# One seven-product stage for both output products, with the final norm's rows staged in DRAM

## Chip, cores and metric

One core of a Trainium2 chip runs the whole program. The metric is device microseconds of one execution; lower is better. All matrices are float32; a factor of a product is split into a high part (rounded to float32r) and a low part, and a product is the sum of high x high, high x low and low x high.

## The reference, cut to what matters

For 1024 prompt tokens and 32 sample tokens (T = 1056 columns; D_MODEL = 2048), the last steps of the layer and of the trunk are

```python
mixed = jnp.concatenate([att * jax.nn.silu(ga), ssm * jax.nn.silu(gs)], axis=-1)
h = h + mixed @ w_out                        # 2048 x 2048
e = _rmsnorm(pe @ w_pe, g_pe)                # made earlier, unscaled, kept as eT in DRAM
h = h + e * jax.nn.sigmoid(h @ w_pg)         # 2048 x 2048
y = _rmsnorm(h, g_final)                     # over the 2048 features of each token
```

Earlier stages (input projection, attention, state space, the embedding's product and the GLU) are not changed.

## The kernel before

Activations lie feature-major: a panel is 128 features by 1056 tokens. Engines run their own instruction lists and wait for each other's semaphores; each list is in the written order, DMA queues included.

**stage_mix** (line 2578) makes h = x + mixed @ w_out. The 2048 input features are halved in two groups of eight *passes* (`NPM` = 8), each group using one half, and each pass makes one pair of 128-row blocks of h (256 output features, `mix_pair`). Inside a pass the 2 x 2 block product (features in two quarters of 512, tokens in two halves of 528) is made as seven block products in place of eight, with sums of weight blocks (`sums`) and of activation blocks. One block product (`product`, line 2751) is 4 x 3 x 2 = 24 matmuls of 264 columns, into the PSUM regions X, B and Y. The seven *sides* (activation factors, 128 x 2112 each) lie split in `m_t_act`; the seven weight factors of a pass are made on the fly in a ring of four. In the loops over `p` (pass) and `j` (slot, 0 to 6) ScalarE casts factor n + 3 (`high`), VectorE makes its sum n + 4 and its low part n + 3 (`sums`, `low`), and both empty PSUM regions (`seed_*`, `keep_*`, `drain_*`, `u2`, `c11`, `c22`, `c12`).

Passes 0 to 7 are opening: they leave partial blocks in `m_zb`, SP stores six of the eight pairs to `cT`. Passes 8 to 15 are closing: they take the partial blocks up again (POOL's `load_part`, line 2722), `residual` adds x from `m_x_res` in four steps, and POOL's `store_h` writes h to `hT`. POOL also moves the *rides*: for the second half of the features, rows of mixT come to `m_ride`, VectorE subtracts (`subtract_rides`), and the differences are stored to `tS`. At the change from pass 7 to 8 POOL reloads each side as soon as its last product is over (`reload_side`), ScalarE casts it (`high_side`, slot n + 3) and VectorE makes its low part (`low_side`, slot n + 4).

**stage_output** (line 3048) has the tokens in two parts, 0 to 511 and 512 to 1055. All 16 panels of h of a part are kept split (`h_hi`, `h_lo`). For each of 16 output tiles of w_pg TensorE runs 16 x 3 matmuls per chunk (`tile`, line 3182; one chunk of 512 columns in part 0, two of 272 in part 1). ScalarE takes the sigmoid, VectorE `gate` scales e by g_pe and e_rstd, multiplies and adds h (rejoined by POOL from the two parts), TensorE transposes the tile (`turn`), ScalarE sums squares (`squares`), VectorE writes it with g_final to token rows (`fill`). When a part is through, `tail` makes rstd, scales the rows and they are stored: part 0's while part 1 computes, part 1's at the very end.

Of the kernel before, what the change touches and what calls it, by code (L numbers as in the profile page):

```python
# [61 lines left out]
RING_H, EARLY_H = 6, 6  # L62
# [50 lines left out]
class Weights:  # L113


    def __init__(self, sb, sem, name, kt, shared=None, before=0):


        self.kt, self.kh, self.before = kt, kt // 2, before
        self.raw, loaded = shared or ([sb(f"{name}_raw{h}", [P, self.kh, P]) for h in range(2)], None)  # L120
        self.hi = [sb(f"{name}_hi{b}", [P, kt, P], F32R) for b in range(2)]
        self.lo = [sb(f"{name}_lo{b}", [P, kt, P], F32R) for b in range(2)]
        self.loaded = loaded or [sem(f"{name}_loaded{h}") for h in range(2)]
# [11 lines left out]
    def split_tile(self, dve, nc, n, b, in_use):  # L135
# [3 lines left out]
        for h in range(2):  # L139
            dve.wait_ge(self.loaded[h], (n + (self.before + 1)) * 16)  # L140
            nc.vector.tensor_copy(self.hi[b][:, h * self.kh:(h + 1) * self.kh], self.raw[h][:]) \
              .then_inc(self.hi_done, 1)
# [5 lines left out]


def prefetch(sp, shared, w, col):  # L150

    raw, loaded = shared
    kh = KD // 2
    for h in range(2):
        sp.dma_start(raw[h][:], w[0].rearrange("(k p) n -> p k n", p=P)[:, h * kh:(h + 1) * kh, col:col + P]) \
          .then_inc(loaded[h], 16)
# [2412 lines left out]

def mix_count(p):  # L2570
    return 16 * (p - NPM + 1)


def mix_pair(p):
    return (p + KEPT) % NPM if p < NPM else p - NPM


def stage_mix(nc, d, G):


    with ExitStack() as ctx:  # L2581
        sb, ps, sem = allocators(nc, ctx)
        pad = sb("m_pad", [P, P // 2])
        t_act, w_raw = sb("m_t_act", [P, 7, 2, KQ, HN], F32R), G["m_raw"]
        W, out = G["W"], G["out"]
        s3 = sb("m_s3", [P, KQ, P])
        w_hi = [sb(f"m_hi{s}", [P, KQ, P], F32R) for s in range(RING_W)]
        w_lo = [sb(f"m_lo{s}", [P, KQ, P], F32R) for s in range(RING_W)]
        zb = [sb(f"m_zb{b}", [P, 4, HN]) for b in range(2)]
        x_res, ride = sb("m_x_res", [P, 4, HN]), sb("m_ride", [P, 4, HN])  # L2590
        acc = ps("m_acc", [P, 6, 512])
# [3 lines left out]
        raw_loaded = {**G["m_blocks"], **{n: sem(f"m_{n}_loaded") for n in ("b12_again", "b22", "b21")}}  # L2595
# [7 lines left out]
            sem(f"m_{n}") for n in ("added", "ridden", "x_loaded", "h_added", "order"))  # L2603
        z_stored = [sem(f"m_z_stored{b}") for b in range(2)]
# [3 lines left out]
        RELOADED = [MOVED + 16 * (1 + n) for n in (2 * NRIDE, NRIDE, NRIDE, 0, NRIDE, 0, NRIDE)]  # L2608
        block = ctx.enter_context(nc.Block(no_gpsimd_drain=True))

        w_out = d["w_out"][0].rearrange("(k p) n -> p k n", p=P)
        mixT = d["mixT"].rearrange("(k p) t -> p k t", p=P)
        hT = d["hT"].rearrange("(k p) t -> p k t", p=P)
        last = 2 * NPM - 1
        DONE = ((0, c11_done), (3, c22_done), (1, c12_done), (2, c21_done))

        def block_of(panel, kh, th):
# [873 lines left out]
```

## Time and profile before

| | us |
|---|---|
| median of 3 runs (2363.88 to 2371.13) | 2366.49 |
| the profiled execution | 2364.5 |
| its span | 2362.5 |
| stage_mix, first to last product | 1583.2 to 1932.9 |
| stage_output, first matmul to last product's end | 1935.8 to 2334.4 |
| after it, to the end of the span | 28.1 |
| TensorE busy, of the span | 93% |
| VectorE, ScalarE, GpSimd busy | 68%, 38%, 13% |

Times inside the profile are counted from the start of the span. The profiled execution's own time is 2.0 us more than its span. TensorE's granted clock has two levels, 2.4 GHz (1.00 in the rows) and 1.2 GHz (0.50), and a stretch shows their mean. Busy time of matmuls overlaps, since they are pipelined: the distance between starts is what one costs.

### The profile page before, as it was taken

What the parts mean: (1) busy time and instruction counts of PE and PEld (TensorE: products, weight loads), DVE (VectorE), ACT (ScalarE), POOL (GpSimd) and SP (SyncE); (2) the same over time, 40 slices, a digit from 0 to 9 for tenths busy, and PEclk for the clock granted to TensorE, in tenths of its full rate; (3) what the DMA queues carried; (4) which work ended last, traced back from release to release, by engine and by line L of the source; (5) the groups of instructions that cost most, each with busy time, mean ns of one, the idle gap of its engine ahead of it and who ended that gap; (6) DMA issues with size and microseconds to landing.
All of it is one profiled execution on the core that took longest, in us unless ns stands there. A gap on an engine that the chain in (4) does not pass through costs nothing. (4 is left out here: it accounts for less than half of the span.)

```text
span 2362.5 us, 44125 instructions
## 1 busy us (share of the span) xinstructions
PE 2202.1 (93%) x16355; PEld 2110.7 (89%) x16355; DVE 1615.5 (68%) x2941; ACT 904.8 (38%) x1843; POOL 315.2 (13%) x412
## 2 busy tenths in 40 slices
PE   3999999999999999999789978978999999999995
PEld 3899999999999999999778868978999988889995
DVE  6779766767787887886456646667566566666663
ACT  6442333333533333334366736234353331123112
POOL 0011000000011212111153410001101211111110
PEclk7999999999999999999989989989999999999998
DMA  8484444444657878786377655464554675445332
GB/s 247 139 269 113 145 139 124 151 124 142 217 182 207 233 215 238 209 242 166 113 245 222 205 181 182 129 207 150 205 195 162 219 246 164 116 118 185 105 97 98
DMA packets 360527, 416.14 MB, mean 176 GB/s; under 512 B 75744, under 2 KB 294472, under 8 KB 352992
## 3 DMA queue, kind: packets, MB, share of 16 engines
q1 hardware_dynamic: 306096, 263.34, 37.9%
q0 software_dynamic: 28224, 106.10, 13.1%
q10 hardware_dynamic: 26032, 44.35, 5.7%
q8 instruction: 112, 1.84, 0.3%
q14 instruction: 63, 0.52, 0.1%
HBM read 265.68 MB, written 139.35 MB: 171 GB/s over the span
## 5 line engine op out<-in xcount | busy, mean ns | idle before, releaser
L767 PE MATMUL acc<-t_act,w_hi 128*128 128x264 f32 x5376 | 886.6, 287 | 9.1 <-DVE zb L1329 5.8
L767 PEld LDWEIGHTS acc<-t_act,w_hi 128*128 128x128 f32 x5376 | 747.4, 189 | 15.5 <-issue 14.1
L767 PE MATMUL acc<-t_act,w_lo 128*128 128x264 f32 x2688 | 547.8, 285 | 0.0
L767 PEld LDWEIGHTS acc<-t_act,w_lo 128*128 128x128 f32 x2688 | 417.0, 189 | 0.0
L2777 PE MATMUL m_acc<-m_t_act,m_hi 128*128 128x264 f32 x1792 | 296.4, 288 | 14.2 <-ACT m_acc L2820 9.8
L1322 DVE TENSOR_TENSOR w_lo<-w_raw_f,w_hi 128x512 fp32r<-128x512 f32 x288 | 197.9, 687 | 133.9 <-ACT w_hi L977 133.5
L977 ACT CAST w_hi<-w_raw_f 128x512 fp32r<-128x512 f32 x288 | 177.9, 618 | 267.7 <-PE acc L767 239.2
L2777 PEld LDWEIGHTS m_acc<-m_t_act,m_hi 128*128 128x128 f32 x1792 | 253.0, 191 | 15.1 <-issue 14.9
L3191 PE MATMUL post_acc<-h_hi,w_post_hi 128*128 128x272 f32 (+1 forms) x768 | 211.2, 329 | 5.7 <-PEq L2581 2.8
L3191 PE MATMUL post_acc<-h_hi,w_post_lo 128*128 128x272 f32 (+1 forms) x768 | 209.0, 327 | 0.0
L3191 PE MATMUL post_acc<-h_lo,w_post_hi 128*128 128x272 f32 (+1 forms) x768 | 208.4, 326 | 0.0
L2777 PE MATMUL m_acc<-m_t_act,m_lo 128*128 128x264 f32 x896 | 184.4, 287 | 0.0
L3191 PEld LDWEIGHTS post_acc<-h_hi,w_post_hi 128*128 128x128 f32 x768 | 130.3, 191 | 17.7 <-DVE h_lo L3292 3.2
L2777 PEld LDWEIGHTS m_acc<-m_t_act,m_lo 128*128 128x128 f32 x896 | 140.7, 191 | 0.0
L3191 PEld LDWEIGHTS post_acc<-h_lo,w_post_hi 128*128 128x128 f32 x768 | 130.1, 191 | 11.0
L3191 PEld LDWEIGHTS post_acc<-h_hi,w_post_lo 128*128 128x128 f32 x768 | 129.3, 190 | 11.3
L2951 DVE TENSOR_TENSOR m_lo<-m_raw,m_hi 128x512 fp32r<-128x512 f32 x96 | 66.0, 688 | 56.3 <-ACT m_hi L2804 56.3
L3245 ACT ACTIVATE junk<-y_ps 128x128 f32<-128x128 f32 (+1 forms) x144 | 37.0, 274 | 172.7 <-PE y_ps L3179 172.7
L3306 DVE TENSOR_TENSOR h<-h,gate_sig 128x512 f32<-128x512 f32 (+1 forms) x32 | 22.7, 709 | 108.5 <-ACT gate_sig L3238 108.5
L661 POOL DMA_DIRECT2D zT<-zb x80 | 43.3, 542 | 342.2 <-DVE zb L1338 145.5
L3141 POOL TENSOR_TENSOR total<-h_hi,h_lo 128x512 f32 (+3 forms) x32 | 50.0, 1565 | 287.3 <-DVE h L3309 277.0
L2804 ACT CAST m_hi<-m_raw 128x512 fp32r<-128x512 f32 x96 | 59.2, 620 | 64.4 <-PE m_acc L2777 61.2
(435 smaller groups left out, 3620.0 us busy)
## 6 DMA issues: line engine op xcount, KB each, us to landing
w_raw_f<-in_w_in_dram SPq DMA_DIRECT2D x96, 512.0 KB, 4.0
w_raw<-in_w_pg_dram SPq DMA_DIRECT2D x64, 512.0 KB, 4.7
cT<-zb SPq DMA_DIRECT2D x22, 1056.0 KB, 4.3
zb<-cT POOLq DMA_DIRECT2D x88, 264.0 KB, 6.2
zT<-zb POOLq DMA_DIRECT2D x80, 264.0 KB, 3.6
m_raw<-in_w_out_dram SPq DMA_DIRECT2D x32, 512.0 KB, 5.6
eT<-e_out ACTq DMA_DIRECT2D x16, 528.0 KB, 3.1
m_x_res<-xT SPq DMA_DIRECT2D x8, 1056.0 KB, 6.2
```

The costliest lines, as they stand in the source:

```text
L661: pool.dma_start(d["zT"][row:row + P, tok:tok + HN], zb[b][:, i]).then_inc(z_put[i], 16)
L767: mm = pe.matmul(out[:, c, 0:QN], w[:, k, :], t_act[:, SIDE[r], x, k, c * QN:(c + 1) * QN], start=(opens and k == 0 and m == 0), stop=(k = ...
L977: nc.scalar.copy(w_hi[n % RING_W][:], factor(p, r)).then_inc(hi_done, 1)
L1322: TT_(w_lo[n % RING_W][:], factor(n // 7, n % 7), w_hi[n % RING_W][:].bitcast(F32), ALU.subtract) \
L2777: mm = pe.matmul(out[:, c, 0:QN], w[:, k, :], t_act[:, MSIDE[r], x, k, c * QN:(c + 1) * QN], start=(opens and k == 0 and m == 0), stop=(k ...
L2804: nc.scalar.copy(w_hi[n % RING_W][:], factor(p, r)).then_inc(hi_done, 1)
L2951: TT_(w_lo[n % RING_W][:], factor(n // 7, n % 7), w_hi[n % RING_W][:].bitcast(F32), ALU.subtract) \
L3141: nc.gpsimd.tensor_tensor(total[b][:, 0:WIDTH[part]], row(hi, part, m).bitcast(F32), row(lo, part, m).bitcast(F32), ALU.add).then_inc(tota ...
L3191: mm = pe.matmul(acc[b][:, c, 0:width], w[:, k, :], a[:, k, start:start + width], start=(k == 0 and n == 0), stop=(k == KD - 1 and n == 2))
L3245: s = nc.scalar.activation(junk[0:rows, t], tr_ps[b][0:rows, t * P:(t + 1) * P], ACT.Square, accum_out=ssq[0:rows, t, bass.ds(m, 1)])
L3306: nc.vector.tensor_tensor(h2[b][:, 0:w], h2[b][:, 0:w], sig[b][:, 0:w], ALU.mult).then_inc(e_gated, 1)
```

## The change

`stage_output` is gone. `stage_mix` runs 32 passes: 0 to 15 as before with w_out, 16 to 23 opening and 24 to 31 closing with w_pg and sides made of h (`block_of`: mixT for c < 2, hT above). The opening and closing roles follow `mix_opens(p)`.

- The sides change three times (before passes 8, 16 and 24). For the latter two `high_side` stands in slot n + 4 and `low_side` in n + 5. Rides happen in passes 1 to 4, 11 to 14 and 17 to 20, and are loaded and stored by SP instead of POOL; `subtract_rides` stands in slot 6.
- h sums go to `x_res`, which is doubled, and hT is stored from there, not from `zb`. The block X of a closing pass comes to its own buffer `x_part`. `load_part` and `store_h` go block by block, in turn.
- In passes 16 to 23 e is loaded, scaled by g_pe and e_rstd (`scale_e`) and stored back to eT; in passes 24 to 31 it is loaded again with h as residual.
- In passes 24 to 31 the four blocks get a sigmoid, a multiply and an add (`gate`); nine token tiles of 256 features are turned in five steps, three to six slots later (`turn`, `squares`, `fill`). The rows of the first six pairs go to `yS` in DRAM (`store_tiles`, ScalarE's queue) and come back in two DMAs in the last pass; those of the last two stay in SBUF.
- All nine token tiles are scaled and stored at the end, five by VectorE and SP, four by ScalarE.
- At the start of the stage `seed_y(0)` stands before the last three sides; the difference for side 6 is made in slot 1 from a second copy of the block, and sides 4, 5, 6 are split in slots 0, 1, 3. The first w_pg tile is no longer loaded ahead into a shared buffer.

```diff
-                    if p == 0 and j < 3:
-                        low_side(4 + j, 4 + j)
+                    if p == 0 and j == 0:
+                        low_side(4, 4)
+                    if p == 0 and j == 1:
+                        dve.wait_ge(raw_loaded["b21_again"], 16)
+                        TT_(first_side[6], ride[:], first_side[2], ALU.subtract).then_inc(t_sub, 1)
+                        low_side(5, 5)
+                    if p == 0 and j == 3:
+                        low_side(6, 6)
...
-                    for s in range(7):
-                        if 7 * p + j == 7 * (NPM - 1) + s + 4:
-                            low_side(7 + s, s)
+                    for c in range(1, 4):
+                        for s in range(7):
+                            if 7 * p + j == 7 * (c * NPM - 1) + s + (4 if c == 1 else 5):
+                                low_side(7 * c + s, s)
...
+                    if 2 * NPM <= p < GATE and j == 5:
+                        scale_e(p)
+                    if p > GATE and j < 2:
+                        gate(p - 1, j + 1)
+                    if p > GATE and j == 1:
+                        gate(p - 1, 3)
+                    if p > GATE + 1 and j < 2:
+                        fill(p - 2, j + 3)
+                    if p > GATE and j >= 4:
+                        fill(p - 1, j - 4)
+                    if p >= GATE and j == 6:
+                        gate(p, 0)
...
+            def turn(p, f):
+                at = fill_at(p, f)
+                pe.wait_ge(h_added, done_count(p, 2 if f < 2 else 3))
+                if at >= 2:
+                    pe.wait_ge(y_filled, at - 1)
+                    pe.wait_ge(squared, at - 1)
+                x = x_res[p % 2].rearrange("p (m h) t -> p m (h t)", m=2)
+                for a, t in enumerate(FILLS[f]):
+                    rows = tile_rows(t)
+                    for m in range(2):
+                        tr = pe.transpose(oth[0:rows, at % 2, (2 * a + m) * P:(2 * a + m + 1) * P],
+                                          x[:, m, t * P:t * P + rows], ident[:])
+                tr.then_inc(turned, 1)
+
+            for p in range(4 * NPM):
                 for r in range(7):
+                    if p > GATE and r >= 3:
+                        turn(p - 1, r - 3)
+                    if p > GATE + 1 and r == 0:
+                        turn(p - 2, 4)
                     product(p, r)
...
+            for s in range(7):
+                reload_side(1, s)
             for p in range(NPM, 2 * NPM):
+                if p == 2 * NPM - 1:
+                    reload_side(2, 0)
+                    reload_side(2, 1)
+                if NPM + KEPT <= p + 1 < 2 * NPM:
+                    load_part(p + 1, 3)
+                for n in range(4):
+                    if NPM + KEPT <= p + 1 < 2 * NPM and n < 3:
+                        load_part(p + 1, n)
+                    if p > NPM:
+                        store_h(p - 1, n)
+            for s in range(2, 7):
+                reload_side(2, s)
...
+            for g in range(3):
+                sp.wait_ge(tiles_put[g], 16 * (NPM - 2))
+            for k, r in ((0, 1), (3, 4)):
+                sp.wait_ge(prod_done, 7 * last + r + 1)
+                sp.dma_start(y_all[:, k:k + 3].rearrange("p k t c -> p k (t c)"),
+                             d["yS"][k:k + 3].rearrange("k p x -> p k x")).then_inc(y_back, 16)
```

## Rows read from the trace of the kernel before

**Rows 1.** The page's busy times, share of the span, instructions: TensorE and VectorE.
```profile
PE 2202.1 (93%) x16355; PEld 2110.7 (89%) x16355; DVE 1615.5 (68%) x2941; ACT 904.8 (38%) x1843; POOL 315.2 (13%) x412
```
**Rows 2.** The page's chain that ended last, shares of the span by line.
```profile
PE post_acc L3191 16%; PE m_acc L2777 12%; PE y_ps L3179 1%; DVE m_t_act L2905 0%; DMA m_t_act<-mixT 0%; ACT m_t_act L2791 0%; DVE m_lo L2951 0%; DMA hT<-m_zb 0%; DVE h_lo L2991 0%; DVE m_zb L3008 0%; DVE w_post_lo L146 0%; DVE m_ride L3004 0%; POOL out_dram L3108 0%; DVE h_lo L3292 0%; ACT junk L3245 0%
```
**Rows 3.** Windows: both stages, the side change, a closing pass, the last stores.
```profile
core 0: us, PE busy (x) PEld busy (x) DVE busy (x) ACT busy (x) POOL busy (x), PEclk, DMA share, GB/s
1583.20:1932.90 349.70, 335.53 (x2690) 334.45 (x2689) 231.42 (x311) 133.87 (x208) 45.84 (x84) 0.97 0.56 193
1935.80:2334.40 398.60, 392.31 (x2443) 355.52 (x2443) 248.39 (x296) 78.74 (x340) 53.27 (x36) 0.98 0.43 130
1748.00:1770.00 22.00, 21.52 (x175) 21.16 (x174) 16.63 (x17) 17.35 (x19) 3.52 (x6) 1.00 0.95 362
...
1824.00:1846.00 22.00, 22.00 (x182) 22.00 (x181) 13.29 (x21) 6.82 (x12) 4.30 (x8) 1.00 0.60 207
2343.30:2355.00 11.70, 0.00 (x0) 0.00 (x0) 1.01 (x1) 1.77 (x1) 1.03 (x2) 0.50 0.98 378
```
**Rows 4.** Waits from 1583 to 1936 us: who for whom, total, times, longest.
```profile
ACT m_acc L2809 <- DMA m_zb<-cT: 25.3, 6, 5.2
...
PE m_acc L2777 <- ACT m_acc L2820: 9.8, 1, 9.8
...
PE m_acc L2777 <- DVE m_zb L2958: 3.9, 1, 3.9
...
PE post_acc L3191 <- PEq L2581: 2.8, 1, 2.8
```
**Rows 5.** Groups by form, 1933 to 2362.5 us: busy, mean ns, idle before.
```profile
L3321 DVE TENSOR_TENSOR y_tok<-y_ps,g_bc 128x512 f32 x24 | 16.6, 692 | 24.6 <-ACT junk L3245 24.6
```
**Rows 6.** Groups by form, 1758 to 1933 us: the sides and the casts.
```profile
L2804 ACT CAST m_hi<-m_raw 128x512 fp32r<-128x512 f32 x47 | 28.9, 620 | 32.3 <-PE m_acc L2777 32.3
...
L2905 DVE TENSOR_TENSOR m_t_act<-m_t_act 128x2112 fp32r<-128x2112 f32 x7 | 16.5, 2350 | 0.0
...
L2791 ACT CAST m_t_act<-m_t_act 128x2112 fp32r<-128x2112 f32 x5 | 9.8, 1970 | 1.7 <-DMA m_t_act<-mixT 1.7
```
**Rows 7.** Timelines at the side change: TensorE, then VectorE (start, duration, what).
```profile
1778.55 0.72 PE L2777 MATMUL m_acc<-m_t_act,m_hi 128*128 128x264 f32 x4 [3.88 <-DVE m_zb L2958]
...
1780.75 1.08 PE L2777 MATMUL m_acc<-m_t_act,m_hi 128*128 128x264 f32 x4
...
1783.78 0.65 PE L2777 MATMUL m_acc<-m_t_act,m_hi 128*128 128x264 f32 x4
...
1775.43 2.35 DVE L2905 TENSOR_TENSOR m_t_act<-m_t_act 128x2112 fp32r<-128x2112 f32 x1
1777.70 0.70 DVE L2958 TENSOR_TENSOR m_zb<-m_acc,m_zb 128x528 f32<-128x528 f32 x1
1778.32 0.68 DVE L2951 TENSOR_TENSOR m_lo<-m_raw,m_hi 128x512 fp32r<-128x512 f32 x1
```
**Rows 8.** Timeline of TensorE where part 0 ends and part 1 begins.
```profile
2126.12 0.39 PE L3191 MATMUL post_acc<-h_hi,w_post_hi 128*128 128x512 f32 x1
2126.35 0.39 PE L3191 MATMUL post_acc<-h_lo,w_post_hi 128*128 128x512 f32 x1
...
2128.56 0.41 PE L3191 MATMUL post_acc<-h_lo,w_post_hi 128*128 128x272 f32 x2
2128.81 0.41 PE L3191 MATMUL post_acc<-h_hi,w_post_lo 128*128 128x272 f32 x2
```
**Rows 9.** Timeline of the tail: rstd, and VectorE's three scaled tiles.
```profile
2340.42 0.19 DVE L3339 RECIPROCAL rstd_y<-std_y 128x5 f32<-128x5 f32 x1 [0.29 <-ACT std_y L3251]
...
2340.65 3.67 DVE L3343 TENSOR_SCALAR y_tok<-y_tok,rstd_y 128x2048 f32<-128x2048 f32 x3
```
**Rows 10.** DMA issues from 1748 to 1802 us: size, median us to landing.
```profile
m_t_act<-tS POOLq DMA_DIRECT2D x4, 1056.0 KB, 7.4
```

More of the change, by code:

```diff
@@ L2660, in load_w, with put_landed @@
                     sp.wait_ge(s_done, 4 * p)
[L2661 to L2662 removed]
+                s, k, col = raw_slot(p, h), p // NPM % 2 * 2 * KQ + h * KQ, mix_pair(p) * 2 * P
+                w = w_out if p < 2 * NPM else w_pg
+                sp.dma_start(w_raw[s][:], w[:, k:k + KQ, col:col + 2 * P]).then_inc(w_loaded[s], 16)
+            def put_landed(p):
+                for i in range(4):
+                    sp.wait_ge(z_put[i], PUT + mix_count(p))
@@ L2688, in _ @@
-            for b in range(2):
-                sp.wait_ge(z_stored[b], 16 * (NPM - KEPT) // 2)
+                    load_residual(NPM)
+                    load_residual(NPM + 1)
+                    with nc.allow_non_contiguous_dma("per-feature columns of the gain"):
+                        sp.dma_start(g_pe[:], d["g_pe"][0].rearrange("(k p) -> p k", p=P)).then_inc(gains_loaded, 16)
+                if ride_of(p - 1):
+                    store_ride(*ride_of(p - 1))
+                if NPM + 2 <= p < 2 * NPM:
+                    put_landed(p - 2)
+                    load_residual(p)
@@ new lines, in _ @@
+                    if p > GATE and j == 0:
+                        sigmoid(p - 1, 2)
+                    if p > GATE + 1 and j == 0:
+                        squares(p - 2, 4)
+                    if p > GATE and j >= 3:
+                        squares(p - 1, j - 3)
+                    for g, (q, slot) in enumerate(((1, 6), (2, 1), (2, 2))):
+                        if GATE <= p - q < last - 1 and j == slot:
+                            store_tiles(p - q, g)
+                    for c in range(1, 4):
+                        for s in range(7):
+                            if 7 * p + j == 7 * (c * NPM - 1) + s + (3 if c == 1 else 4):
+                                act.wait_ge(sides_moved[s], reloaded(c))
+                                high_side(7 * c + s, s)
@@ L3022, in _ @@
                         c22(p)
-                    if p == last and j == 6:
-                        for k in range(EARLY_H):
-                            low_h(k)
                     if j == 6:
@@ new lines, in _ @@
+            fill(last - 1, 3)
+            gate(last, 1)
+            gate(last, 2)
+            fill(last - 1, 4)
+            gate(last, 3)
+            for f in range(5):
+                fill(last, f)
+            nc.vector.reduce_sum(var[:], ssq[:], axis=AX_X).then_inc(var_summed, 1)
+            dve.wait_ge(var_summed, 1)
+            nc.vector.tensor_scalar(var[:], var[:], 1.0 / D_MODEL, EPS, ALU.mult, ALU.add).then_inc(var_done, 1)
+            dve.wait_ge(std_done, 1)
+            nc.vector.reciprocal(rstd[:], std[:]).then_inc(rstd_done, 1)
```

764 lines of the change are left out of this document (313 added, 451 removed).

## The prediction

> **What bounds the kernel now.** I read first the page's busy times, then its chain of waits: TensorE is busy 93% of the span, and the chain that ended last is mostly TensorE, 16% of the span on line 3191 (the product with w_pg) and 12% on line 2777 (the product with w_out) [rows 1, 2]. Then the stages [rows 3]. The seven-product stage runs from 1583.2 to 1932.9 us, the w_pg stage from 1935.8 to 2334.4, and after it 28.1 us of tail hold almost no TensorE work. In both stages TensorE is busy 96 to 98% of the time at a granted clock of 0.97 to 0.98 (2.4 GHz most of the time), so fewer matmul columns mean less time until something else is late. The waits [rows 4] and the two timelines [rows 7, 9] give what that costs where it already happens.
>
> **The product itself.** Before: part 0 is 16 tiles x 48 matmuls of 512 columns, 768, which start 0.231 us apart (0.23 and 0.23 between the rows); part 1 is 16 x 96 = 1536 of 272 columns, two in 0.25 us, 0.1255 each [rows 8]. That is 177.4 + 192.8 = 370.2 us. 144 transposes at about 0.12 us (five start within 0.6, an estimate from a 128-wide matmul's share of the 272-wide one's 0.1255) are 17, and the remaining 11 of the stage's 398.6 are its start at the low clock and waits for h_lo.
> After: 16 passes of 7 products of 24 matmuls of 264 columns. In a pass of the stage before, 182 matmuls start in 22 us [rows 3] (the row 1824 to 1846), one per 0.121 to 0.122. A pass is 168 x 0.1222 = 20.5 us, a product ("slot" below) 2.93, sixteen passes 328.5. The same 144 transposes are there, but 126 fall between products (18 a pass in the last seven), and the last 20 in the tail: 14 us. Together 342.5. The idle 2.8 us between the blocks goes as well [rows 4]. So TensorE's part falls by 398.6 + 2.8 - 342.5 = 58.9 us. Everything below takes back from this.
>
> **Two more changes of the side operands.** Each new group of eight passes reloads seven sides of 1056 KB; each costs ScalarE 1.97 us and VectorE 2.35 [rows 6]. The trace has one such change, at pass 8: the seven VectorE pieces, 16.5 us, put it behind, and TensorE stood 3.9 us until u2 was done [rows 4, 7]; then groups of four matmuls took 1.08 us in place of 0.65 for about 4 us [rows 7], about 2 us more. So one change costs 6 to 6.5 us today, and the kernel keeps that one. At the two new ones low_side stands a slot later (n + 5, before n + 4), so a side is finished two slots before its product and not three. Counting VectorE by starts (0.60 to 0.62 us from one 512 or 528 wide operation to the next, 2.27 after a side, where the durations are 0.68, 0.70 and 2.35 [rows 7]):
> At pass 16 the slots from (15,5) to the c22 of (16,5) hold seven sides 15.9, seven lows 4.3, four sums 2.4, two evacuations 1.4, four residuals 2.5 and that c22 0.7, 27.2 us, against eight slots, 23.4 us. Product 6 is 3.8 us late, with the clock about 6. Four POOL stores of h now stand between the side loads, which also wait for the last ride store, and ride, x, h and side bytes together are about 11.9 MB in a pass of 20.5 us, while the one change seen ran at 0.95 DMA share and 362 GB/s [rows 3]. I take 8, bounds 4 (the late products hidden as partly as at pass 8) and 15 (the loads late by three slots).
> At pass 24 there are also scale_e (two 1056-wide operations, 2.6 in all, an estimate from the 0.70 of a 528-wide one [rows 7]), add_parts 1.9, u2 and c11 1.4, and no residual: 30.7 us for the same eight slots, 7.2 late. The gaps come in several pieces, each with a stretch at the low clock: I take 11, bounds 6 and 22 (twice what I count, if ScalarE, which waits in order for a side's landing of 7.4 us [rows 10], holds back its casts and so VectorE).
> Of TensorE's clock the Trainium skill says the same in "TensorE: Matmul & The Clock Gate" ("HAM oscillation"): each return to work after an idle stretch is paid at the lower clock. Our rows agree (3.9 us idle, then about 4 us of 1.08 us groups); by that rule many pauses of a few us would be dearer than one of their sum, and it is the reason for the upper bound.
>
> **The eight passes with the gate.** Per pass VectorE gets: seven lows 4.3, four sums 2.4, four evacuations 2.5, four gates of two operations 5.2, and fills of nine row tiles 2.9 (512-wide 0.69 [rows 5], the 256-wide ones about 0.4). 17.3 us of a pass of 20.5 + 2.0. ScalarE: seven casts 4.3 (0.62 each [rows 6]), evacuations and seeds 3.0, three sigmoids 1.8, squares about 3.5, 12.6 in all. Neither is full. Slot by slot: slots 0 and 1 carry two and four gate halves more than they have room for (about 2.6 us behind at the end of slot 1), slot 2 has one operation, and u2 of slot 3 is in time. Transposes f + 2 wait for fill f, which ends 2.6 to 2.8 us into a slot of 2.93 + 0.5. So nearly no stall, but it's tight: I take 2 us, bounds 0 and 20 (0.6 us at each of 35 turns).
> DMA of a gate pass: w 1.05, h 1.08, e 1.08, cT 1.08 and staged rows 1.18 MB, 5.5 MB in 22.5 us, 243 GB/s; a pass now runs at 207 with a share of 0.60 [rows 3], so 0.7. Nothing there. Passes 17 to 20 (w, cT, e in and out, rides in and out) need 6.4 MB, 312 GB/s, share 0.9. scale_e may wait there a few us; it is last in its slot, low is three slots ahead, so nothing for TensorE.
> The split of residual and hT stores (x_res doubled, x_part) removes a wait of ScalarE for cT, 25.3 us over six [rows 4]. In the steady passes TensorE was full already [rows 3]: nothing gained. The rides move from POOL to SP: SP waits there for things that are done by slot 4, its weight loads have seven slots; nothing.
>
> **The start.** TensorE waits 9.8 us for seed_y of pass 0, queued behind a high_side that waits for the third difference [rows 4]. Now seed_y is ahead, and two of the 2112-wide VectorE operations come behind products 3 and 4. Laid out by VectorE durations, product 6 of pass 0 ends 3.8 us earlier, but the one gap becomes four of 0.5 to 2.4, some at the low clock. I take -2, bounds -5 and +3.
>
> **The tail.** Today 6.0 us from the last matmul to rstd, then scaling, and the data flow from 2343.3 to 2355.0 at 378 GB/s: 4.46 MB, rows 512 to 1055 [rows 3, 9]; the others were stored at half time under matmuls. Then 7.5 us to the end. Afterwards all 8.65 MB go out at the end: 4.19 MB more at 378 is 11.1 us. rstd comes later by about 3.3: the last gate half, then five chained turn, squares and fill steps in two banks in place of one. The scaling isn't the bound: VectorE makes a tile in 1.22 us [rows 9]. The reload of six passes' rows, 7.1 MB, begins when product 1 of the last pass is over and ends about when rstd does. The new block ends without the GpSimd drain, -2. Sum +12, bounds +6 (the 7.5 us mostly go) and +20 (reload late by 6, 300 GB/s).
> The Trainium skill, "DMA: Bandwidth & Descriptors" ("Where 436 GB/s comes from"), lets about 358 GB/s of HBM traffic bind. The row has 378; by the page the extra bytes would take 11.7 us, 0.6 more.
>
> **Sum.** -58.9 + 8 + 11 + 2 - 2 + 12 = -27.9 us. The profiled execution took 2364.5 us (span 2362.5), so 2336.6; it lies 2.0 below the median of 2366.49, so I give 2338.
>
> **The rivals.**
> A. Everything at its lower bound: the changes hide as the one at pass 8 does, and the end overhead goes. -58.9 + 4 + 6 + 0 - 5 + 6 = -48, 2318. For it: nothing else than TensorE is above 68% busy. Against: VectorE is over its slots by count at both changes.
> B. DMA holds the changes and the tail: both upper bounds, 15 + 22, and 20 for the tail: -58.9 + 37 + 2 - 2 + 20 = -2, 2364, no change; half of that, 2352. For it: 0.95 share at the change seen. Against: that change cost only 3.9 us though the queues were full.
> C. Slower: the order between TensorE and VectorE in the gate passes. Product r stands behind turn f, turn behind fill f - 2, fill behind a low that waits for ScalarE's cast, which stands behind squares and sigmoids. If one such round trip misses its slot, all do: TensorE then waits in each of 35 turns, and falls to 1.2 GHz for stretches. At 0.8 us a turn it costs 28 us and the gain is gone; at 1.2 us, 42, 2378. For it: 2.8 of 3.4 us used by my count. Against: slots 2 and 3 leave VectorE about 2 us of room each pass.
> D. The change doesn't do what it says, sixteen passes but with products held at 1.2 GHz or passes far over 22.5 us for another reason: no row speaks for it; part of C.
>
> **How the numbers follow.** My forecast, 2328 to 2348: 0.48. A, below 2328: 0.15. B, 2348 to 2359: 0.18 faster, 0.06 no change. C: 0.13, of which 0.12 slower and 0.01 no change. Within 0.3% is 2359.4 to 2373.6, about what a measurement of this kernel can tell from none. Faster 0.81, same 0.07, slower 0.12. The range 2316 to 2364 leaves out a part of A and nearly all of C.
>
> **What would show it.** TensorE's passes 16 to 31 at 20.5 us, and 22.5 with turns; idle of 3 to 8 us once near the start of each of passes 16 and 24, ahead of r = 4 to 6, released by VectorE; the first wait of 9.8 us replaced by three short ones; from the last product to the first store 11 to 13 us and then some 23 us of full DMA. Wrong would be: waits of transposes on the gate or fill in every pass, idle at the changes released by DMA, or TensorE time per pass above 23.

## The result and the profile after

The changed kernel takes 2376.26 us (median of 4 runs, 2374.82 to 2378.66), the kernel before 2365.18 beside it (4 runs, 2363.42 to 2371.13): ratio 1.0044, 95% interval 1.0027 to 1.0062. It is slower, by 11 us; the forecast was 2338 and the range ended at 2364. The profiled execution took 2374.8 us, its span is 2373.1.

The page of the kernel after, busy times and the chain that ended last; they answer to [rows 1, 2]:
```profile
PE 2172.8 (92%) x16739; PEld 2110.0 (89%) x16739; DVE 1652.8 (70%) x3049; ACT 1001.8 (42%) x1862; POOL 269.0 (11%) x387
...
PE 14%; DMA 7%; DVE 7%; issue 2%; SPq 2%; ACT 1%; POOL 0%; ACTq 0%; DVEq 0%; POOLq 0%
PE m_acc L2930 13%; DMA tS<-m_ride 3%; DMA m_ride<-hT 2%; SPq L2761 2%; DVE m_t_act L3135 2%; DVE m_lo L3181 1%; DMA m_ride<-mixT 1%; PE m_oth L2945 1%; DMA m_t_act<-tS 1%; DVE m_zb L3151 1%; DVE m_s L3172 0%; DMA m_e_res<-eT 0%; ACT m_y_out L3121 0%; DVE m_ride L3141 0%; DVE m_ride L3142 0%
```
TensorE is still busy 92% of the span. But in the chain its share fell, and right behind its own line stand the two ways of a ride, `tS<-m_ride` and `m_ride<-hT`, and SP's issue of the ride's stores (SPq L2761). None of these three stands among the lines that the chain of before shows, and the forecast had given them nothing.

The windows of the kernel after, for [rows 3]: passes 0 to 15, passes 16 to 31, then passes 3 to 5, 14 and 15, 16, 19 to 22, 24, the gate pass 26, and the last stores (most windows lie up to 2 us behind the first product of their pass; after the times: busy us of each engine, TensorE's granted clock, DMA share, GB/s):
```profile
core 0: us, PE busy (x) PEld busy (x) DVE busy (x) ACT busy (x) POOL busy (x), PEclk, DMA share, GB/s
1585.00:1952.80 367.80, 342.85 (x2702) 339.01 (x2702) 237.39 (x321) 134.73 (x205) 36.03 (x65) 0.97 0.59 203
1952.80:2336.84 384.04, 350.33 (x2801) 346.85 (x2800) 273.77 (x384) 168.78 (x351) 20.19 (x37) 0.98 0.70 256
...
1656.90:1733.10 76.20, 67.33 (x510) 66.36 (x509) 38.83 (x58) 20.81 (x37) 0.00 (x0) 0.93 0.56 190
1905.40:1952.80 47.40, 42.86 (x340) 41.53 (x339) 32.83 (x49) 14.01 (x22) 9.57 (x17) 1.00 0.76 262
1952.80:1987.50 34.70, 23.31 (x171) 22.41 (x170) 26.28 (x25) 19.34 (x21) 2.90 (x6) 0.90 0.76 294
2029.00:2133.80 104.80, 88.31 (x676) 86.81 (x675) 62.22 (x85) 27.54 (x48) 0.00 (x0) 0.95 0.68 245
2154.30:2181.80 27.50, 21.67 (x170) 20.76 (x169) 26.79 (x28) 16.64 (x21) 0.43 (x1) 1.00 0.66 245
2204.30:2227.00 22.70, 22.70 (x190) 22.68 (x189) 17.79 (x30) 12.01 (x35) 2.14 (x4) 1.00 0.69 250
2350.00:2366.00 16.00, 0.00 (x0) 0.00 (x0) 4.06 (x4) 6.14 (x4) 0.00 (x0) 0.50 1.01 417
```
What the reader is to see: passes 3 to 5 moved only 190 GB/s at a DMA share of 0.56, and still took some 76 us where three plain passes take 61.7. A closing pass of the kernel before moved 207 GB/s without a loss [rows 3], so the bytes alone don't explain it; run 3 tries order against bytes. The gate pass has no idle TensorE at all.

Each pass by the starts of its products. A plain pass took 20.55 us, a gate pass 22.47; all 5376 product matmuls are in the trace, so a pass is known to 0.1. The account in spans, after less before, beside the terms of the forecast:

| term | forecast | measured |
|---|---|---|
| the product, worked out again from nine passes of 20.55 and seven of 22.47 | -58.9 | -59.2 |
| start (pass 0) | -2 | -3.8 |
| passes 3 to 5 (28.4, 26.1, 21.4), rides of change 1 | 0 | +14.2 |
| passes 14 and 15 (24.1, 23.1) | 0 | +6.2 |
| pass 16 (34.7), second change of sides | +8 | +14.2 |
| passes 19 to 22 (30.0, 26.0, 25.5, 23.1), rides of change 3 | 0 | +22.5 |
| pass 24 (27.5), third change of sides | +11 | +7.0 |
| turns and gates | +2 | 0 |
| tail, from the last product's end | +12 | +8.0 |
| passes 7 and 8, and a later start of the stage | 0 | +1.8 |
| sum | -27.9 | +10.9 (spans: +10.6) |

How a ride makes a pass long. VectorE's and SP's waits in passes 1 to 5 of the kernel after:
```profile
DVE m_raw L3163 <- DMA m_raw<-in_w_out_dram: 23.0, 5, 5.6
DVE m_ride L3140 <- DMA m_ride<-mixT: 21.3, 3, 10.7
...
SPq L2785 <- DVE m_zb L3152: 79.0, 6, 15.2
SPq L2752 <- DMA tS<-m_ride: 9.4, 3, 4.4
```
And SP's and VectorE's timelines (start, duration, what, idle before):
```profile
1673.58 0.33 SPq L2785 DMA_DIRECT2D cT<-m_zb  x1
1674.00 0.38 SPq L2740 DMA_DIRECT2D m_raw<-in_w_out_dram  x1
1674.43 4.55 SPq L2761 DMA_DIRECT2D tS<-m_ride  x4
1679.02 1.02 SPq L2740 DMA_DIRECT2D m_raw<-in_w_out_dram  x1
1683.04 0.81 SPq L2752 DMA_DIRECT2D m_ride<-mixT  x2
...
1666.16 0.71 DVE L3140 TENSOR_TENSOR m_ride<-m_ride 128x528 f32<-128x528 f32 x1 [10.68 <-DMA m_ride<-mixT]
1690.52 0.71 DVE L3140 TENSOR_TENSOR m_ride<-m_ride 128x528 f32<-128x528 f32 x1 [6.02 <-DMA m_ride<-mixT]
1713.64 0.71 DVE L3140 TENSOR_TENSOR m_ride<-m_ride 128x528 f32<-128x528 f32 x1 [4.59 <-DMA m_ride<-mixT]
```
A ride is a closed ring through one buffer. From one difference to the next: 2.9 us of differences, 4.5 until SP may issue the cT store, which waits for add_parts of the next pass (line 3152), 0.9 for cT and a weight load, 4.6 for the issue of the four stores, 4.1 with the next weight load until they have landed, 0.8 for two loads, and 6.7 until VectorE goes on: 24.4 us between 1666.16 and 1690.52, against a plain pass of 20.55. From the first difference of one ride to that of the next the trace has 31.3, 24.4 and 23.1 us in change 1, 24.3, 24.0 and 24.1 in change 2, and 31.0, 25.8 and 25.7 in change 3. VectorE stands in slot 6 for what is missing; behind it in its order are `sums` and `low` of the coming products, so TensorE stands too, and part of the 23.0 us for the weights is the same stall, since their loads are issued behind those stores.

### The profile page after: what moved, and what is told of

The parts are those of the page before. It is cut to its first block and busy times, and to the rows that moved or that the text cites. A ratio compares the mean times of both kernels' runs of the same rounds, so it can differ in the third digit from the quotient of the medians.

```text
span 2373.1 us, 44712 instructions
## 1 busy us (share of the span) xinstructions
PE 2172.8 (92%) x16739; PEld 2110.0 (89%) x16739; DVE 1652.8 (70%) x3049; ACT 1001.8 (42%) x1862; POOL 269.0 (11%) x387
## 2 busy tenths in 40 slices
DMA packets 331078, 477.63 MB, mean 201 GB/s; under 512 B 78912, under 2 KB 250280, under 8 KB 321088
## 5 line engine op out<-in xcount | busy, mean ns | idle before, releaser
L757 PEld LDWEIGHTS acc<-t_act,w_hi 128*128 128x128 f32 x5376 | 749.1, 189 | 15.5 <-issue 14.2
L2930 PE MATMUL m_acc<-m_t_act,m_hi 128*128 128x264 f32 x3584 | 599.8, 290 | 58.7 <-DVE m_lo L3181 14.7
L2930 PEld LDWEIGHTS m_acc<-m_t_act,m_hi 128*128 128x128 f32 x3584 | 507.1, 192 | 65.9 <-issue 34.2
L2930 PE MATMUL m_acc<-m_t_act,m_lo 128*128 128x264 f32 x1792 | 369.7, 288 | 0.0
L2930 PEld LDWEIGHTS m_acc<-m_t_act,m_lo 128*128 128x128 f32 x1792 | 282.8, 192 | 0.0
L2978 ACT CAST m_hi<-m_raw 128x512 fp32r<-128x512 f32 x192 | 118.8, 620 | 174.8 <-PE m_acc L2930 101.8
L3181 DVE TENSOR_TENSOR m_lo<-m_raw,m_hi 128x512 fp32r<-128x512 f32 x192 | 131.4, 687 | 56.4 <-ACT m_hi L2978 56.3
L2244 DVE CUSTOM_DVE_ANT_0 prob<-score,negc_bc 128x128 f32<-128x128 f32 (+8 forms) x72 | 53.4, 750 | 30.8 <-PE score L2017 29.5
L2268 DVE TENSOR_TENSOR pt_lo<-turned,pt_hi 128x512 fp32r<-128x512 f32 (+2 forms) x112 | 52.8, 508 | 27.2 <-ACT pt_hi L2160 25.4
L2149 ACT ACTIVATE prob<-prob,stat 128x128 f32<-128x128 f32 (+8 forms) x72 | 56.1, 781 | 21.8 <-DVE stat L2244 14.9
L3135 DVE TENSOR_TENSOR m_t_act<-m_t_act 128x2112 fp32r<-128x2112 f32 x23 | 54.1, 2352 | 0.0
```

The costliest lines, as they stand in the source:

```text
L757: mm = pe.matmul(out[:, c, 0:QN], w[:, k, :], t_act[:, SIDE[r], x, k, c * QN:(c + 1) * QN], start=(opens and k == 0 and m == 0), stop=(k = ...
L2149: e = nc.scalar.activation(prob[s % 4][:, col:col + width], prob[s % 4][:, col:col + width], ACT.Exp, scale=-1.0, bias=stat[b][:, n, 0:1], ...
L2244: z = nc.vector.tensor_tensor_reduce(out=prob[s % 4][:, col:col + width], in0=score[b][:, col:col + width], in1=negc[hb][:, row:row + widt ...
L2268: c = nc.vector.tensor_tensor(out, src, hi.bitcast(F32), ALU.subtract)
L2930: mm = pe.matmul(out[:, c, 0:QN], w[:, k, :], t_act[:, MSIDE[r], x, k, c * QN:(c + 1) * QN], start=(opens and k == 0 and m == 0), stop=(k ...
L2978: nc.scalar.copy(w_hi[n % RING_W][:], factor(p, r)).then_inc(hi_done, 1)
```

## The experiments

Every ratio is against the kernel before in the same rounds. Where nothing else is said, a base is the changed kernel.

**1. no_rides.** Rides of changes 1 and 3 left out.
```diff
-        FIRST_RIDE = {1: 1, 2: NPM + 3, 3: 2 * NPM + 1}
+        FIRST_RIDE = {2: NPM + 3}
```


> Leaves out the rides of the first and third side change (no loads, no four differences, no stores to tS; sides 1, 2, 4, 6 of passes 8 to 15 and 24 to 31 are then not the right ones); those of the second stay. The changed kernel lost 14 us in passes 3 to 5 and 22 us in passes 19 to 22 against 20.55 us a pass. Theory 1 (the chain of one ride, subtract in slot 6, add_parts, cT store, weight load, four stores issued by SP, landing, two loads, landing, takes longer than a pass): both groups fall to 20.6 us a pass, -34 us, 2342. Theory 2 (too many bytes for the DMA queues): the same here, -34. Theory 3 (e's way out and back is what holds passes 19 to 22): only -14, 2362.


Measured: 2338.3 us, 0.9878 (0.9862 to 0.9895). Passes 3 to 5 and 19 to 22 are all at 20.55. The 36.7 us of the two groups are the rides.

**2. pool_rides.** Those rides through POOL, which loads, waits for the difference and stores; the differences stay in slot 6.
```diff
+            for r in range(NRIDE):
+                move_rides(1, r)
```


> The rides of the first and third change go through POOL's queue, as they did for the first change in the kernel before; the same bytes, and the differences stay in slot 6. Theory 1: a ride's chain loses the wait behind add_parts, the cT store and the weight load, and the 4.6 us that SP takes to issue four stores; it becomes 3 (differences) + 2.2 + 5 + 1.1 + 5 = 16 us, under a pass of 20.5: -25 to -34 us, 2342 to 2351. Theory 2 (bytes): nothing, 2376. Theory 3: -14.


Measured: 2353.4, 0.9942 (0.9925 to 0.9959). Off SP's queue, the rides cost 23 us less than in the changed kernel: pass 2 at 24.5, 3 at 21.3, 19 to 21 at 22.5, 23.5, 21.6. What is left is no longer a wait for a ride: before each first difference VectorE now stood 0.0 us. From 1638 to 1685 us it stood 12.5 us for two weight loads, 7.1 us for one of them; they landed 12.5 us (median) after their issue, beside the two residuals (13.4). So without SP's queue the ring no longer holds VectorE. The 11 us that these passes still lose look like transfers that crowd one another, a share of the bytes; that wasn't tried by itself.

**3. sp_shift.** The differences in slot 2 of the next pass, the stores behind the weight load that follows; still SP.
```diff
                 load_w(p + 2, 0)
+                if ride_of(p - 1) and ride_of(p - 1)[0] in (1, 3):
+                    store_ride(*ride_of(p - 1))
...
-                    if j == 6 and ride_of(p):
+                    if j == 6 and ride_of(p) and ride_of(p)[0] not in (1, 3):
                         subtract_rides(*ride_of(p))
+                    if j == 2 and ride_of(p - 1) and ride_of(p - 1)[0] in (1, 3):
+                        subtract_rides(*ride_of(p - 1))
```


> The rides of the first and third change stay in SP's queue, but the differences move from slot 6 of the pass to slot 2 of the next and the stores stand behind the next weight load instead of before x, e and that load. Same bytes, same queue. Theory 1: the chain is 3 + 4.6 + 4 + 0.8 + 6.5, 19 to 20 us, just under a pass, and a late ride meets a slot with room: -20 to -30 us, 2346 to 2356. Theory 2: nothing, 2376. Theory 3: -14.


Measured: 2349.4, 0.993 (0.9913 to 0.9946), 27 us less than the changed kernel with the same instructions and bytes. Passes 3 to 5 come to 20.6. Its VectorE timeline at the first difference of each ride has no more waits after the first:
```profile
1671.50 0.71 DVE L3142 TENSOR_TENSOR m_ride<-m_ride 128x528 f32<-128x528 f32 x1 [3.63 <-DMA m_ride<-mixT]
...
1688.40 0.70 DVE L3142 TENSOR_TENSOR m_ride<-m_ride 128x528 f32<-128x528 f32 x1
...
1708.96 0.70 DVE L3142 TENSOR_TENSOR m_ride<-m_ride 128x528 f32<-128x528 f32 x1
```
The bytes and the queue are the same, and the bytes theory had said 2376: it is refuted for these passes. Slot 2 of the next pass is also where the kernel before had its differences. The move of the differences and the move of the stores were not tried apart. One wait of 6 us was left, and pass 19 took 27.7.

**4. no_e.** scale_e and the way of e to eT and back left out in passes 16 to 23.
```diff
-                    if 2 * NPM <= p < GATE and j == 5:
-                        scale_e(p)
```


> Leaves out scale_e and e's load and store in passes 16 to 23 (e then goes unscaled into the gate); 2.16 MB and 2.5 us of VectorE less per pass. Theory 1: passes 19 to 22 keep most of their 22 us, since the ride chain is unchanged, and pass 24 gets 2 to 3 us shorter: -3 to -8 us, 2368 to 2373. Theory 2 (bytes): 6.4 MB a pass become 4.3, the 22 us go: -25, 2351. Theory 3: the same, -25; passes 3 to 5 are unchanged in every theory.


Measured: 2364.0, 0.9987 (0.9977 to 0.9998), 12 us less, between theory 1 (3 to 8) and the other two (25). Passes 20 to 23 fall to 20.5 to 21.0, pass 19 only from 30.0 to 28.9, passes 3 to 5 by 1.1 us in all, pass 24 from 27.5 to 25.1. So 13.6 of the 22.5 us in passes 19 to 22 appear only with e, more than theory 1 gave. The differences of change 3 still follow one another at 28.8, 23.1 and 21.6 us, where they had 31.0, 25.8 and 25.7: e's traffic lengthens the ring by 2 to 4 us a round, and without e it is still longer than a pass. Pass 24 lost 2.4 us, and scale_e takes VectorE 2.55 a pass: the first sign of what sets pass 24.

**5. gpe_late.** The element-wise load of g_pe leaves pass 2.


> The changed kernel with one edit: the element-wise load of g_pe leaves pass 2 of the stage and is issued in pass 9; it then no longer stands on SP's queue right ahead of the first ride's four stores, which took SP 10.5 us to issue behind it in the changed kernel. Theory 1 (a ride's chain of waits through SP is longer than a pass, and passes 3 to 5 are long for it; the gain load makes the first link longer by some 6 us): pass 3 falls from 28.35 to 22 to 25 us, passes 4 and 5 stay at about 26 and 21.4, because rides 1 to 3 follow one another at the same distance; in all 2370 to 2373. Theory 2 (the bytes of passes 2 to 4 fill the DMA engines, whichever queue holds them): nothing moves, 2376. Rival 3 (everything late in passes 3 to 5 is a consequence of the late first link): all of the 14 us go, 2362.


Measured: 2374.4, 1.0036 (1.0021 to 1.005): 2 us less at most, pass 3 at 27.1. The ride's first four stores now took 2.1 us to issue and not 10.5, yet the next load of a ride was issued at 1659.63 us, before at 1660.24:
```profile
1644.11 1.98 SPq L2770 DMA_DIRECT2D m_x_res<-xT  x2
1646.18 2.13 SPq L2761 DMA_DIRECT2D tS<-m_ride  x4
...
1659.63 0.81 SPq L2752 DMA_DIRECT2D m_ride<-mixT  x2
```
My reading of the 10.5 us as the cause of pass 3 is refuted. The load of the next ride waits for the landing of the stores. Here they landed 10.1 us (median) after their issue, right behind two residuals of 1056 KB that took 10.3 us; whether the residuals are the cause wasn't tried.

**6. c2_order.** On sp_shift: the residual's load ahead of the ride stores, POOL's stores of h ahead of the first two side reloads; the rides of change 2 themselves as they were.
```diff
-                if ride_of(p - 1):
-                    store_ride(*ride_of(p - 1))
                 if NPM + 2 <= p < 2 * NPM:
                     put_landed(p - 2)
                     load_residual(p)
+                if ride_of(p - 1) and ride_of(p - 1)[0] not in (1, 3):
+                    store_ride(*ride_of(p - 1))
...
-                if p == 2 * NPM - 1:
-                    reload_side(2, 0)
-                    reload_side(2, 1)
...
                         store_h(p - 1, n)
+                    if p == 2 * NPM - 1 and n in (1, 3):
+                        reload_side(2, n // 2)
```


> The kernel with the shifted rides of changes 1 and 3 (2349.4, passes 14, 15 and 16 of 24.5, 22.6 and 34.0 us), with two changes of order around the second change of sides and not a byte less: SP loads the residual of a pass ahead of the four stores of the ride, and POOL stores the four blocks of h of pass 14 ahead of the first two reloads of sides, where the second reload waited 15 us for the last ride. Order theory: VectorE's waits for m_x_res (3.8 and 3.7 us) go, passes 14 and 15 come to 20.6 to 21.5, pass 16 loses the pile of side loads and h stores at 1948 to 1953 us and comes to 28 to 31; in all 2338 to 2343. Bytes theory (rides, x, h and sides together saturate the engines in passes 14 to 16): the losses stay in sum and only move between the passes, 2347 to 2351.


Measured: 2358.2, 0.9953 (0.9937 to 0.997): 9 us more than its base. Passes 13 to 15 grew to 23.4, 27.8 and 26.3. A miss, and VectorE's waits from 1872 to 1952 us, this kernel's first, then the changed kernel's, say why:
```profile
DVE m_ride L3141 <- DMA m_ride<-hT: 20.4, 3, 7.6
...
DVE m_x_res L3217 <- DMA m_x_res<-xT: 3.0, 2, 1.7
```
```profile
DVE m_x_res L3216 <- DMA m_x_res<-xT: 10.9, 4, 3.8
...
DVE m_ride L3140 <- DMA m_ride<-hT: 6.2, 3, 2.1
```
The wait for the residual went, and a dearer one for the ride came: a load of 1056 KB now stood inside the ride's ring, whose differences follow at 27.6, 27.0 and 24.9 us. POOL's edit comes only in pass 15, so it can't be what made passes 13 and 14 longer. I had mended the wait that showed, not the ring it hid.

**7. slots3.** On sp_shift: the sides of changes 2 and 3 a slot earlier.
```diff
-                            if 7 * p + j == 7 * (c * NPM - 1) + s + (3 if c == 1 else 4):
+                            if 7 * p + j == 7 * (c * NPM - 1) + s + 3:
...
-                            if 7 * p + j == 7 * (c * NPM - 1) + s + (4 if c == 1 else 5):
+                            if 7 * p + j == 7 * (c * NPM - 1) + s + 4:
```


> The kernel with the shifted rides (2349.4, passes 16 and 24 of 34.0 and 29.0 us), with high_side and low_side of changes 2 and 3 in slots +3 and +4, as change 1 has them, in place of +4 and +5. If VectorE's slots set the loss at a change, as the prediction counted (a side ready two slots ahead of its product and not three; 3.8 and 7.2 us late), each of passes 16 and 24 becomes 2 to 4 us shorter: 2342 to 2346. If the landing of the seven side loads sets it, the earlier slot only moves the wait to ScalarE, which then holds back its casts one slot earlier: no change or up to 4 us longer, 2349 to 2353.


Measured: 2353.7, 0.9943 (0.9926 to 0.9959), against 2349.4 (0.993) in its base. Pass 24 is 29.8 (28.9), pass 16 34.8 (34.0). So the later slot, which the prediction gave as a reason for its larger terms, costs nothing. The time agrees with the expectation's landing theory, but in pass 24 TensorE's one long wait (5.5 us) is for VectorE; run 13 decides it.

**8. all_order.** The edits of runs 5, 6 and 7 together on sp_shift, and the rides of change 3 in passes 18 to 21.


> Everything of this round together on the shifted rides: g_pe loaded in pass 9, residual ahead of the ride stores, h stores ahead of the reloads, side slots +3 and +4, and the rides of change 3 one pass later (18 to 21), where the one wait of 6 us for the first of them stood in pass 19. Not a byte less than the changed kernel moves. Order theory: passes 3 to 5 and 19 to 23 at 20.6 to 21, passes 14 and 15 at 21, 16 at 28 to 31, 24 at 25 to 28: 2330 to 2338, below the run that left the rides out (2338.3). Bytes theory: 2345 to 2350.


Measured: 2355.6, 0.995 (0.9934 to 0.9967). A miss as a sum, since it holds c2_order's loss; but passes 19 and 20 are at 20.6. That part stands alone in the next run.

**9. ride3_late.** On sp_shift.
```diff
-        FIRST_RIDE = {1: 1, 2: NPM + 3, 3: 2 * NPM + 1}
+        FIRST_RIDE = {1: 1, 2: NPM + 3, 3: 2 * NPM + 2}
```


> The kernel with the shifted rides of changes 1 and 3 (2349.4), its side slots as in the changed kernel, with one edit: the rides of change 3 happen in passes 18 to 21 and not 17 to 20. In the run with four orders changed together this removed the one wait of 6 us for the first of them (pass 19 from 27.8 to 20.5). Order theory: pass 19 at 20.5 to 21, pass 24 at 28 to 30 as before: 2341 to 2344. If the bytes of passes 17 to 22 were the limit, the 6 us come up in another of passes 20 to 24: 2347 to 2350.


Measured: 2340.8, 0.9893 (0.9876 to 0.9909). Pass 19 falls from 27.7 to 20.6, and passes 20 to 23 stay at 20.6. Rides and e's traffic now share passes 18 to 22 for nothing.

**10. c2_none.** On ride3_late, rides of change 2 left out.


> As the run before it (rides of change 3 in passes 18 to 21), and the rides of change 2 are left out: the sides 1, 2, 4 and 6 of the second change are reloaded from what the first change left there. It bounds what those rides cost in passes 13 to 16. Theory 1 (the rides, by POOL's wait of 15 us for the last of them and the pile of loads behind it): passes 14 and 15 at 20.6, pass 16 at 27 to 29, as pass 8 has with its rides done: 12 to 14 us less than the run before it, 2328 to 2332. Theory 2 (the stores of h, the residuals and the seven sides, with VectorE's four residual adds on top): pass 16 stays at 32 to 34, and only 5 us go, 2337 to 2339.


Measured: 2325.4, 0.983 (0.9814 to 0.9847), 15.4 us less: passes 13 to 15 at 20.5, pass 16 at 26.6 and not 34.6. So 8.0 of pass 16 go with the rides, and 6.1 don't.

**11. c2_shift.** On ride3_late: all rides with the difference in slot 2 of the next pass and the stores behind the weight load, only the last of change 2 ahead of it; c2_order's two moves as well.
```diff
-                if ride_of(p - 1):
-                    store_ride(*ride_of(p - 1))
                 if NPM + 2 <= p < 2 * NPM:
                     put_landed(p - 2)
                     load_residual(p)
+                if ride_of(p - 1) == (2, NRIDE - 1):
+                    store_ride(*ride_of(p - 1))
...
                 load_w(p + 2, 0)
+                if ride_of(p - 1) and ride_of(p - 1) != (2, NRIDE - 1):
+                    store_ride(*ride_of(p - 1))
```


> As the run with the rides of change 3 in passes 18 to 21, and the rides of change 2 are shifted like the others: the differences in slot 2 of the next pass, the stores behind the weight load (those of the last ride ahead of it, since a side waits for them), SP's residual loads ahead of the ride stores, POOL's four stores of h ahead of the first two side reloads. No byte less. The run with the last two alone was 9 us slower: there the differences stayed in slot 6, and VectorE stood 7.6, 7.0 and 5.8 us for the rides' loads. Order theory: those waits go, passes 13 to 15 at 20.6 to 22, pass 16 at 30 to 33 (the last ride is stored as late as before): 2334 to 2340. Bytes theory: passes 13 to 16 stay at their sum of 102 us or more, 2342 to 2350.


Measured: 2328.9 us (2327.4 to 2332.9), 0.9847 (0.983 to 0.9864). The same operations as in the changed kernel, the same 477.63 MB, 47 us less; it beats both kernels and is the version to keep. The differences of change 2 now follow at 20.4 us, the length of a pass. Its windows: passes 0 to 15, from the middle of pass 1 to that of pass 5, passes 14 and 15, and 16:
```profile
1585.00:1931.30 346.30, 335.81 (x2699) 334.26 (x2698) 238.36 (x321) 133.90 (x204) 35.03 (x63) 0.98 0.63 217
...
1625.50:1708.00 82.50, 81.67 (x668) 81.48 (x667) 51.09 (x75) 26.84 (x48) 0.00 (x0) 1.00 0.65 220
1890.10:1931.30 41.20, 41.20 (x341) 41.20 (x340) 29.95 (x44) 13.79 (x22) 6.31 (x11) 1.00 0.87 297
1931.30:1964.00 32.70, 23.30 (x173) 22.58 (x172) 26.54 (x26) 19.65 (x21) 4.04 (x8) 0.90 0.77 298
```
Passes 14 and 15 now move 297 GB/s at a share of 0.87 with TensorE at 41.20 of 41.20 us, where the changed kernel moved 262 at 0.76 and stood. The bytes theory is refuted for these passes.

**12. half_out.** The changed kernel without ScalarE's four final stores (4.19 MB).


> The changed kernel (2376.3), with ScalarE's four final stores left out (four of the nine token tiles, 4.19 MB of 8.65; they are still scaled). It sizes the tail, where the prediction took 11.1 us for exactly these bytes more. If the bytes set the end, at the 411 to 426 GB/s of the tail's windows: 10.0 us less, 2366; at the 378 GB/s of before: 11.1, 2365. If the scaling by VectorE (1.2 us a tile, five tiles) or the end's fixed part takes part, 3 to 8 us less, 2368 to 2373.


Measured: 2363.7, 0.9989 (0.998 to 0.9999), 12.6 us less by the medians and 11.3 by the spans (2373.1 and 2361.8). From the last product's end to the end of the span it is 25.3 us and not 36.0, 10.7 less, where the prediction priced these bytes at 11.1. At 417 GB/s they are 10.1 us. The rest of the difference lies ahead of the tail and isn't explained.

**13. side_few.** On c2_shift, all but 16 of 528 columns of the side loads of changes 2 and 3 left out.
```diff
-                pool.dma_start(plain(s), src)
+                part = (slice(0, P), slice(None), slice(0, HN if c == 1 else 16))
+                pool.dma_start(plain(s)[part], src[part])
```


> The kernel with all rides shifted (2328.9; pass 16 at 32.7 us, pass 24 at 28.3), with the fourteen side loads of changes 2 and 3 cut to the first 16 of 528 token columns of each of four feature rows (left out: 97% of these loads' 14.8 MB; every cast and difference of the sides stays, on old data). It sizes the terms '8' and '11', which the prediction worked out from VectorE's slots alone. VectorE theory: pass 24 stays at 27 to 28.5, since ScalarE waited for a side's landing only 0.7, 0.5 and 0.2 us there; pass 16, where it waited 9.8 us once, comes to 27 to 28; in all 2322 to 2324. Landing theory: both passes fall to 21 to 24, 2313 to 2318.


Measured: 2326.6, 0.9826 (0.981 to 0.9842). Pass 24 comes from 28.3 to 27.5, pass 16 from 32.3 to 25.9: almost without the bytes, 7.0 and 5.3 us stay. VectorE in this kernel, around passes 16 and 24:
```profile
1931.00:1951.00 20.00, 16.69 (x132) 15.98 (x131) 18.61 (x18) 17.11 (x17) 5.59 (x9) 1.00 0.44 145
2108.00:2137.00 29.00, 25.41 (x190) 24.90 (x191) 28.25 (x32) 15.98 (x21) 1.09 (x2) 0.94 0.38 120
```
28.25 of 29.00 us busy at a DMA share of 0.38. On pass 24 alone (2103.9 to 2131.4 us) VectorE is busy 27.43 of 27.50 us, and 27.43 of 27.50 also in the changed kernel (2152.4 to 2179.9). So VectorE sets pass 24. The landing theory holds only for the first products of pass 16, which give 6.5 us here.

**14. resid_early.** On c2_shift, a pass's residual loaded half a pass earlier.


> The kernel with all rides shifted (2328.9), and the load of a pass's residual (1056 KB, passes 10 to 15) is issued half a pass earlier, behind the last weight load of the pass before; in pass 15 it then doesn't stand ahead of the last ride's four stores, which landed 9.4 us after they were issued and held the second side load until then. Order theory: the second side comes 3 to 5 us earlier, the wait of 12.0 us in the first product of pass 16 shrinks to 7 to 9, and pass 16 to 28 to 30: 2324 to 2326. If the loads of the sides one by one set it, as wide as the engines are, nothing: 2328 to 2330.


Measured: 2336.7, 0.9879 (0.9855 to 0.9902), 8 us more. Pass 16 did fall, from 32.3 to 26.7 us, but passes 13 and 15 went to 24.5 and 27.0. The residual again stands ahead of the ride stores, and VectorE waits 7.5 us for two ride loads in passes 12 to 16, where c2_shift has no such wait. The loss moved and grew.

## Why the prediction was wrong

**The step that failed** is one sentence of the prediction: the rides move from POOL to SP, which waits for things that are done by slot 4; nothing. It cost 36.7 us in passes 3 to 5 and 19 to 22 (run 1), 13.6 of them only together with e's traffic (run 4), and the rides of change 2, their differences in slot 6 as well, cost 15.4 with their part in pass 16 (run 10). The prediction counted what each of SP's issues waits for, one by one, and never added up the ring that they close: difference, SP's place behind the cT store, issue, landing, load, landing, next difference. Its sum was to be compared with 20.5 us. Rows for it were there: four operations of 0.7 [rows 7] and two landings, if each takes the 7.4 us of [rows 10], are already 17.6 us (an estimate), before any issue or place on the queue. Runs 3, 9 and 11 take nearly all of these losses away without a byte or an operation less.

The prediction also speaks only of the move from POOL to SP. The same change had moved the differences three slots ahead: the kernel before makes them in slot 2 of the next pass (line 3033, `subtract_rides(p - 1)`), the changed kernel in slot 6 of the same pass. In the kernel before, rides cost nothing: passes 1 to 6 take 20.55 us each, the differences follow at 20.6, and POOL waits for VectorE and not the other way round:
```profile
1649.55 2.15 POOL L2703 DMA_DIRECT2D tS<-m_ride  x4 [10.50 <-DVE m_ride L2913]
1659.84 1.07 POOL L2699 DMA_DIRECT2D m_ride<-mixT  x2 [8.13 <-DMA tS<-m_ride]
1670.11 2.15 POOL L2703 DMA_DIRECT2D tS<-m_ride  x4 [9.20 <-DVE m_ride L2913]
```
Run 2 puts the queue back and keeps the slot, run 3 puts the slot back and keeps the queue (with the stores at another place). Each gets most of the loss back, 23 and 27 us, so the loss comes mostly from the two together.

**The product**: right. 20.55 us a pass and 22.47 in the gate passes, forecast 20.5 and 22.5; -58.9 against -59.2, also at a granted clock of 0.97 to 0.98. The 126 turns between products were put at 14 us, though at 0.12 each they are 15.1; they took 13.4.

**The changes of sides**: 19 in sum, measured 21.2, which is luck, since each is wrong. Pass 24, forecast 11, cost 7.0: that is the prediction's own count of VectorE's lateness, 7.2, and the surcharge for the clock was not there. What pass 16 keeps without rides is 6.1 us (run 10), and 5.3 almost without side bytes (run 13). The forecast had 3.8 by count and 6 with the clock. The 6 fits by luck, since in both runs the granted clock of the pass is 1.00: the count was short by 1.5 to 2.3. The 8.0 us above it go with the rides of change 2; the last of them was stored so late that POOL, which must reload side 1 from it, stood 15 us. In the kernel after:
```profile
1947.77 0.54 POOL L2854 DMA_DIRECT2D m_t_act<-tS  x1 [15.15 <-DMA tS<-m_ride]
1948.30 2.14 POOL L2863 DMA_DIRECT2D hT<-m_x_res  x4
...
1957.06 1.95 ACT L2965 CAST m_t_act<-m_t_act 128x2112 fp32r<-128x2112 f32 x1 [10.78 <-DMA m_t_act<-tS]
```
The prediction saw that the side loads "also wait for the last ride store" and priced it inside its upper bound of 15, which just held. That a later slot makes the change dearer was false (run 7).

The rule on "HAM oscillation" in the Trainium skill ("TensorE: Matmul & The Clock Gate"), the reason for pass 24's upper bound, weighed nothing there: TensorE stood in pieces of at most 2.3 us, the window of pass 24 has a granted clock of 1.00, and the run side_few, at 0.94, has the same 27.5 us. In passes 3 to 5 and 16 it is 0.93 and 0.90, so some of what those stalls cost is the clock's; how much wasn't tried.

**The gate passes and rival C**: no stall, 22.70 us busy of 22.70 in pass 26. Slower came true, but not by C's mechanism: its 0.12 was on the wrong place.

**DMA**: the prediction allowed scale_e a few us in passes 17 to 20 and nothing for TensorE. e does cost, 12 us in all (run 4), mostly by lengthening the ride's ring: this is a second part of the failed step. With the rides one pass later (run 9), e and the rides lie in the same passes for nothing.

**The start**: -3.8, within the bounds of -5 and +3. **The tail**: +12 forecast, 8.0 measured. rstd came 10.6 us after the last product, forecast 9.3 (6.0 + 3.3). The data flow ran at 417 GB/s and not 378. The term for GpSimd's drain was too small: it was put at -2 without a row, and in the trace of the kernel before POOL's DRAIN at the end takes 5.70 us, while in the changed kernel 0.5 us pass from the last landing to the end of the span. All of that was inside the bounds.

Had the rides cost nothing, with everything else as measured, the kernel would have come out near run 10's 2325.4 or run 11's 2328.9, 9 to 13 us under the forecast (an estimate) and inside the range: the other terms were on the whole too careful.

## What to carry to other kernels

A buffer that is loaded, changed, stored and loaded again through several queues in order is a ring, and its period must be added up from start to start, with each queue's place and each landing, before it is called hidden; it then has to be shorter than the loop it rides in. Where it isn't, moving a link to another slot can get the time back without a byte less (here the differences three slots later and the stores behind the weight load). A stall that shows at one wait may belong to a ring that another wait hides: mend the ring first, or the cure lands inside it, as in runs 6 and 14. And compare the slots of before and after line by line: a link that moved without being named in the forecast gets no term there.

## What the runs showed of the hardware

- The final stores of row tiles ran at 417 GB/s over 16 us at a DMA share of 1.01, where the last stores of before had 378 [rows 3]. The section on "Where 436 GB/s comes from" of the Trainium skill ("DMA: Bandwidth & Descriptors"), cited in the prediction, lets about 358 bind; both rows lie above it, so it didn't bind here.
- Behind the 8 KB element-wise load of g_pe, SP's next four issues took 10.49 us in the changed kernel, and 2.13 with that load gone (run 5). Elsewhere the same four took 2.62 to 4.58 us in the changed kernel and 1.96 to 4.96 in sp_shift.
